# Every second weight unit issued by GpSimd through its own DMA queue, in a two-layer conv/MLA trunk with hierarchical MoE

## The chip, the cores and the metric

One core of a Trainium2 chip runs the whole kernel. The core has TensorE (PE in the profile; PEld is its weight load), VectorE (DVE), ScalarE (ACT), GpSimd (POOL) and SyncE (SP), each with its own instruction stream, and sixteen DMA engines that they share. The metric is the time of one execution on the device in microseconds; lower is better.

## What is computed

A token sequence of 256 by 1024 (float32) goes through two layers. Layer 0 is a Conformer convolution module, layer 1 an MLA attention over a shared latent. Each is followed by a mixture of 32 experts in 4 groups, of which a token uses two. The experts are nearly all of the weights, and every expert's weights are read:

```python
def hierarchical_moe(h, norm_g, w_group, b_group, w_router, b_router, w_gate_up, w_down):
    xt = rms_norm(h, norm_g).reshape(B * S, D)
    ...
    def expert_step(acc, ex):
        w_gu, w_d, g = ex
        a, b = jnp.split(xt @ w_gu, 2, axis=-1)
        return acc + ((jax.nn.silu(a) * b) @ w_d) * g[:, None], None

    y, _ = lax.scan(expert_step, jnp.zeros_like(xt), (w_gate_up, w_down, gates.T))
    return y.reshape(B, S, D)
```

`w_gate_up` is 32 x 1024 x 1024 in each layer and `w_down` 32 x 512 x 1024.

## The kernel before

The program is written by hand, engine by engine, with semaphores. Nothing is scheduled by a tool: the order of a queue is the order in the code.

*Units and slots.* The experts of a layer are taken four at a time; such a set is a quad, and there are eight. Each quad's weights come as twelve units of 2 MB: units 0 to 7 are gate_up, 8 to 11 are down. The units of a layer are numbered through, g = 0 to 95. They land in ten slots in SBUF, six in the tensor `ring` and four in `zone`; unit g takes the slot of unit g - 10 in turn. In the first quad, and for the down units of the last, a unit holds 128 weight rows of all four experts and comes in rows of 4 KB (`128x4x1024`). In all others ("blocks") it holds 512 rows of one expert, and each partition gets 16 KB that lie together (`128x4096`).

*Who frees a slot.* TensorE counts the semaphore `used` up. In the first quad it does so after each unit; in blocks it takes units in pairs (0 with 1, 2 with 3, ...) and adds two after a pair. `unit_free` waits for that count:

```python
sp.wait_ge(e["used"], UNITS * n + (u // 2 * 2 + 2 if blocks else u + 1))
```

*The order on SyncE.* Behind the inputs and the convolution's weights, `experts(l, first)` issues 84 units (`EARLY`) in order and then, in a loop `sp.Fori` over a count of rounds that is computed on the device (one, with this routing), the twelve units of the last quad. `first(g)` holds the first ten units back until the memory that they overwrite has been read. In the last quad, units 0 and 1 take the slots of units 6 and 7 of the quad before it, and units 6 and 7 those of this quad's units 0 and 1. Then come the attention weights (L445 to L451) and the same for layer 1.

*TensorE in a quad.* `gate_up` (L845), then `gather` for the next quad (L827), `hidden_across` and `weights_back` (L855, L863), `down` (L879) and `scatter` (L894). In the last quad `down` takes its units one by one.

*GpSimd.* It sets constants and adds up the products of the depthwise convolution (L506, L509). After that it has nothing to do for the rest of the kernel.

Of the kernel before, what the change touches and what calls it, by code (L numbers as in the profile page):

```python
# [14 lines left out]
P = 128  # L15
# [5 lines left out]
SIDE = 4  # L21
# [4 lines left out]
SLOTS = 10  # L26


def trunk_kernel(nc: bass.Bass, a, out):
    _, S, D = a["x"].shape  # L30
    L, NE, _, FF2 = a["w_gate_up"].shape
    F = FF2 // 2
    TT = S // P
# [15 lines left out]
    QUADS = NE // SIDE  # L49
    ROUNDS = QUADS * (PASSES - 1) + 1  # L50
    HALF = 512
    assert TT == 2 and D == 2 * HALF and NOPE == P and DV == P and QUAD == P and KF * P == F and NE == 32

    with ExitStack() as ctx:
        def sb(name, shape, dt=F32):
            return ctx.enter_context(nc.sbuf_tensor(name, shape, dt))

        def sem(name):
            return ctx.enter_context(nc.semaphore(name))
# [7 lines left out]
        unit_sb = [(ring[:, u * UNIT:(u + 1) * UNIT] if u < 6 else zone[:, (u - 6) * UNIT:(u - 5) * UNIT])  # L67
                   .rearrange("p (k c) -> p k c", k=4) for u in range(SLOTS)]
# [60 lines left out]
        slot = sb("slot", [P, TT, NC_])  # L129
        cmx = sb("cmx", [P, 1 + PASSES])  # L130
        rounds_i = sb("rounds_i", [P, 1], I32)
# [60 lines left out]
        def added_count(j):  # L192

            return j + 1 + block_of_buffered[j]

        def sums_done(b):

            return block_of_buffered.index(b) + block_of_buffered.count(b) + b + 1

        def product_buf(i):  # L200

            return spot(2304 + i * S, S) if i < 6 else spot(UNIT + 2048 + (i - 6) * S, S)
# [30 lines left out]
        for loads, at, parts in (  # L233
# [8 lines left out]
            first = at  # L242
# [10 lines left out]
        GU = KD  # L253
        UNITS = KD + KF
        EARLY = UNITS * (QUADS - 1)
# [5 lines left out]
        def slot_of(l, g):  # L261

            return slot_order[l][g % SLOTS]

        def slot_last(l, u):

            return slot_order[l][turn_last[u]]
# [7 lines left out]
        def by_blocks(n):  # L275

            return n != 0
# [49 lines left out]
        pw1_done, sg_ready, u_ready, u_zero = sem("pw1_done"), sem("sg_ready"), sem("u_ready"), sem("u_zero")  # L327
# [3 lines left out]
        mean_done, diff_ready = sem("mean_done"), sem("diff_ready")  # L331
        sq_ready, var_done, lstd_ready, dn_ready = sem("sq_ready"), sem("var_done"), sem("lstd_ready"), sem("dn_ready")
        c_ready, pw2_done, hb_ready = sem("c_ready"), sem("pw2_done"), sem("hb_ready")
# [3 lines left out]
        mask_ready, pos_done, rounds_ready = sem("mask_ready"), sem("pos_done"), sem("rounds_ready")  # L337
        count_done = sem("count_done")

        E = []  # L340
        for l in range(L):
            e = {n: sem(f"{n}_{l}") for n in (
                "gate_done", "used", "half_done", "pick_ready", "pw_ready", "g_done", "xs_ready", "silu_done", "hid_ready",
                "hT_done", "hidT_ready", "back_done", "pwT_ready", "y_ready", "s_done", "s_added")}
# [4 lines left out]
        ang_ready, trig = sem("ang_ready"), sem("trig")  # L349
        c_done, csq, crms_ready, cn_ready = sem("c_done"), sem("csq"), sem("crms_ready"), sem("cn_ready")  # L350
        ctr_done, cT_ready = sem("ctr_done"), sem("cT_ready")
        kvmm_done, kv_evac, qmm_done, q_evac = sem("kvmm_done"), sem("kv_evac"), sem("qmm_done"), sem("q_evac")
# [6 lines left out]
        o_done, o_dve, o_act, wo_done = sem("o_done"), sem("o_dve"), sem("o_act"), sem("wo_done")  # L359
# [6 lines left out]
        def _(sp):  # L366
# [31 lines left out]
            def unit_dma(l, slot, u, ex, blocks):  # L398
                src = a["w_gate_up"][l] if u < GU else a["w_down"][l]
                if blocks:  # L400
                    r0 = (u // SIDE) * HALF if u < GU else 0
                    src = src[bass.ds(ex + u % SIDE, 1), r0:r0 + HALF, :].rearrange("e (p k) c -> (e p) k c", k=4)
                else:
                    r0 = (u if u < GU else u - GU) * P
                    src = src[bass.ds(ex, SIDE), r0:r0 + P, :].rearrange("e p c -> p e c")
                sp.dma_start(unit_sb[slot], src).then_inc(E[l]["unit_in"][slot], 16)

            def unit_free(e, n, u, blocks):

                sp.wait_ge(e["used"], UNITS * n + (u // 2 * 2 + 2 if blocks else u + 1))  # L410

            def experts(l, first):
                e = E[l]
                for g in range(EARLY):
                    if g < SLOTS:
                        first(g)
                    else:
                        unit_free(e, (g - SLOTS) // UNITS, (g - SLOTS) % UNITS, by_blocks((g - SLOTS) // UNITS))
                    unit_dma(l, slot_of(l, g), g % UNITS, SIDE * (g // UNITS), by_blocks(g // UNITS))
                sp.wait_ge(rounds_ready, l + 1)  # L420
                n_last = sp.value_load(rounds_i[0:1, 0:1], min_val=1, max_val=ROUNDS)
                with sp.Fori(0, n_last) as i:
                    for u in range(UNITS):
                        if u in (6, 7):
                            unit_free(e, i + (QUADS - 1), u - 6, True)
                        else:
                            unit_free(e, i + (QUADS - 2), u + 6 if u < 2 else u, True)
                        unit_dma(l, slot_last(l, u), u, (i + (QUADS - 1)) % QUADS * SIDE, u < GU)
                return n_last

            def first_after_conv(g):
# [7 lines left out]
                if g == 8:  # L439
                    sp.wait_ge(pw2_done, 4)  # L440

            last = experts(0, first_after_conv) + (QUADS - 2)

            unit_free(E[0], last, 6, True)
# [8 lines left out]
            def first_after_attention(g):  # L453
# [6 lines left out]
                if g == 4:  # L460
                    sp.wait_ge(wo_done, 4)

            last = experts(1, first_after_attention) + (QUADS - 2)
            out_t = out[0].rearrange("(t p) d -> p t d", p=P)
            for j in range(4):
# [6 lines left out]
        @block.gpsimd  # L472
        def _(pool):
            nc.gpsimd.memset(ident[:, :], 0.0).then_inc(zeroed, 1)
            nc.gpsimd.memset(upto[:, :], 1.0).then_inc(zeroed, 1)
            nc.gpsimd.memset(mask[:, :], 0.0).then_inc(zeroed, 1)
            pool.wait_ge(zeroed, 3)
            nc.gpsimd.affine_select(out=ident[:, :], in_=ident[:, :], compare_op=ALU.not_equal, fill=1.0, base=0,
                                    pattern=[[-1, P]], channel_multiplier=1).then_inc(const_ready, 1)
            nc.gpsimd.affine_select(out=upto[:, :], in_=upto[:, :], compare_op=ALU.is_ge, fill=0.0, base=0,  # L480
                                    pattern=[[1, P]], channel_multiplier=-1).then_inc(const_ready, 1)

            nc.gpsimd.memset(mask[0:CHUNK, S - CHUNK:S], -NEG).then_inc(const_ready, 1)
            nc.gpsimd.memset(ones[:, :], 1.0).then_inc(const_ready, 1)
            nc.gpsimd.memset(eps_c[:, :], EPS).then_inc(const_ready, 1)
            nc.gpsimd.memset(slot[:, :, :], -1.0).then_inc(const_ready, 1)
            nc.gpsimd.iota(iota_i[:, :], pattern=[[1, CAP]], base=0, channel_multiplier=0).then_inc(const_ready, 1)
            nc.gpsimd.memset(u_sb[:, :, 0:PAD], 0.0).then_inc(u_zero, 1)
            pool.wait_ge(small_in, 16)
            pool.wait_ge(xn_ready, 2)  # L490
            for t in range(TT):
                nc.gpsimd.tensor_tensor(h[:, t, :], h[:, t, :], pw2_b_row, ALU.add).then_inc(hb_ready, 1)

            pool.wait_ge(tr_done, 4)
            nc.gpsimd.memset(mean_w, 1.0 / D).then_inc(mean_set, 1)

            made, j = 0, 0
            for b, (m, acc, other, w0) in enumerate(SUMS):
                for i in range(CW - w0):
                    made += 1  # L500
                    if i >= 2:
                        pool.wait_ge(product_ready, made)
                        if i >= 4:
                            pool.wait_ge(pool_added, added_count(j - 2))
                        dst = acc if i % 2 == 0 else other
                        nc.gpsimd.tensor_tensor(dst, dst, product_buf(j % PRODUCTS), ALU.add).then_inc(pool_added, 1)  # L506
                        j += 1
                pool.wait_ge(pool_added, sums_done(b) - 1)
                nc.gpsimd.tensor_tensor(acc, acc, other, ALU.add).then_inc(pool_added, 1)  # L509


        @block.scalar
        def _(act):
# [20 lines left out]

            act.wait_ge(cols_ready, 1)
            made, diags = iter(range(sum(CW - w0 for _, _, _, w0 in SUMS))), iter(range(CW))
            made_buffered = [0]

# [936 lines left out]
```

## Time and profile before

| | |
|---|---|
| median of 3 runs | 1174.38 us (1172.61 to 1174.65) |
| the profiled execution | 1175.39 us, with a span of 1173.7 us from first to last instruction |
| mean granted TensorE clock | 0.971 |
| TensorE busy | 1055.6 us (90%) |
| VectorE, ScalarE, GpSimd busy | 243.8, 168.7, 58.2 us |
| transfers | 430.72 MB, 367 GB/s over the span |

The profile is of one execution. Its times count from the first instruction; what lies around the span, 1.69 us here, is in the execution's time alone. Busy time of an engine says how much it did, not whether the kernel waited for it; for that the stages and the chain of waits are read. Transfers are listed by queue (q1 holds what SyncE issues, q10 what ScalarE issues, q8 and q14 bring instructions).

### The profile page before, as it was taken

The page shows a single profiled execution, that of the slowest core. Times are in us where ns is not written, and L with a number is a line of the kernel's source. Part 1 is how long each engine was busy: PE and PEld are TensorE (multiplying, and loading weights), DVE is VectorE, ACT ScalarE, POOL GpSimd, SP SyncE. Part 2 cuts the span into 40 slices and gives each one's busy share as a digit, 9 for nine tenths or more (in the row PEclk, how much of TensorE's full clock was granted, in tenths as well). Part 3 has the DMA queues.
Part 4 walks back from the last instruction along what each step waited for, and adds up shares of the span by engine and source line. Part 5 has one row for each costly group of instructions (what it writes and reads, how often), then busy time and mean ns, then how long its engine had stood idle before and what let it go on. Part 6 is the DMA issues. An engine that isn't in the chain of part 4 may idle for free.

```text
span 1173.7 us, 11470 instructions
## 1 busy us (share of the span) xinstructions
PE 1055.6 (90%) x4866; PEld 505.6 (43%) x4866; DVE 243.8 (21%) x521; ACT 168.7 (14%) x427; POOL 58.2 (5%) x92
## 2 busy tenths in 40 slices
PE   6999799989898979898999897979898989798988
PEld 5885542424242424242555555424242424242424
DVE  4993411101010100010226314101010101010001
ACT  2775200000000000000236202000000000000000
POOL 2790000000000000000000000000000000000000
PEclk9999799999999999999999897999999999999999
DMA  9683599999999999999975009999999999999996
GB/s 320 183 359 143 215 383 428 428 427 428 429 427 429 428 428 427 428 428 421 385 298 215 1 1 369 421 428 428 428 428 427 427 428 427 428 427 429 427 422 277
DMA packets 63966, 430.72 MB, mean 367 GB/s; under 512 B 12086, under 2 KB 22413, under 8 KB 43180
## 3 DMA queue, kind: packets, MB, share of 16 engines
q1 hardware_dynamic: 63790, 429.86, 88.7%
q8 instruction: 38, 0.62, 0.2%
q10 hardware_dynamic: 126, 0.14, 0.0%
q14 instruction: 12, 0.10, 0.0%
HBM read 428.94 MB, written 1.05 MB: 366 GB/s over the span
## 4 chain that ended last, share of the span: by engine, by line
PE 55%; DMA 39%; DVE 3%; ACT 1%; issue 1%; SPq 0%; ACTq 0%; DVEq 0%
DMA zone<-in_w_gate_up_dram 21%; DMA ring<-in_w_gate_up_dram 18%; PE bank L845 13%; PE bank L827 11%; PE bank L879 10%; PE bank L745 5%; PE bank L1034 2%; PE bank L785 2%; PE bank L967 1%; PE bank L894 1%; PE bank L977 1%; PE bank L757 1%; PE bank L945 1%; ACT xT L610 1%; PE bank L951 1%
## 5 line engine op out<-in xcount | busy, mean ns | idle before, releaser
L845 PE MATMUL bank<-ring,zone 128*32 128x512 f32 x1184 | 327.9, 608 | 39.9 <-DMA ring<-in_w_gate_up_dram 25.9
L845 PE MATMUL bank<-zone 128*32 128x512 f32 x864 | 270.9, 613 | 33.5 <-DMA zone<-in_w_gate_up_dram 18.9
L845 PEld LDWEIGHTS bank<-ring,zone 128*32 128x32 f32 x1184 | 87.6, 112 | 216.2 <-issue 214.9
L879 PE MATMUL bank<-ring,xT 128*32 128x512 f32 x672 | 144.2, 593 | 4.2 <-ACT xT L610 4.2
L827 PEld LDWEIGHTS bank<-zone,xn 128*128 128x128 f32 x576 | 132.5, 324 | 14.1 <-issue 14.1
L845 PEld LDWEIGHTS bank<-zone 128*32 128x32 f32 x864 | 69.7, 113 | 158.9 <-issue 157.9
L827 PE MATMUL bank<-zone,xn 128*128 128x128 f32 x576 | 135.9, 398 | 0.5 <-DVE zone L1229 0.5
L1248 DVE TENSOR_TENSOR xT<-xT,bank 128x512 f32<-128x512 f32 x16 | 11.0, 688 | 474.5 <-PE bank L845 474.5
L879 PE MATMUL bank<-zone,xT 128*32 128x512 f32 x352 | 93.4, 594 | 3.3 <-ACT xT L610 3.3
L608 ACT ACTIVATE xT<-bank 128x512 f32<-128x512 f32 x16 | 9.6, 597 | 549.6 <-PE bank L845 549.6
L1253 DVE TENSOR_TENSOR h<-bank,h 128x512 f32<-128x512 f32 x64 | 44.3, 692 | 210.5 <-PE bank L894 210.5
L879 PEld LDWEIGHTS bank<-ring,xT 128*32 128x32 f32 x672 | 38.0, 110 | 78.2 <-issue 72.4
L894 PE MATMUL bank<-zone,xT 128*128 128x512 f32 x128 | 62.3, 618 | 0.0
L745 PE MATMUL bank<-xT,ring 128*128 128x256 f32 x256 | 58.1, 391 | 0.8 <-issue 0.8
L745 PEld LDWEIGHTS bank<-xT,ring 128*128 128x128 f32 x256 | 50.3, 197 | 8.5 <-issue 1.2
L1132 DVE SCALAR_TENSOR_TENSOR bank<-zone,dwT,bank 128x256 f32<-128x256 f32 x125 | 49.9, 482 | 0.0
L1241 DVE TENSOR_TENSOR zone<-bank,cols 128x512 f32<-128x512 f32 x36 | 24.9, 692 | 109.0 <-PE bank L827 109.0
L879 PEld LDWEIGHTS bank<-zone,xT 128*32 128x32 f32 x352 | 23.6, 110 | 46.2 <-issue 42.0
L618 ACT COPY zone<-bank 128x512 f32<-128x512 f32 x32 | 18.8, 586 | 163.3 <-PE bank L879 163.3
L894 PEld LDWEIGHTS bank<-zone,xT 128*128 128x128 f32 x128 | 20.3, 188 | 42.2 <-DVE h L1253 21.0
L506 POOL TENSOR_TENSOR xn<-xn,zone 128x256 f32<-128x256 f32 x41 | 29.5, 732 | 0.4 <-ACT zone L560 0.4
L1034 PE MATMUL bank<-ring,xT 128*128 128x512 f32 x64 | 27.9, 594 | 1.5 <-ACT xT L704 1.5
(238 smaller groups left out, 624.3 us busy)
## 6 DMA issues: line engine op xcount, KB each, us to landing
ring<-in_w_gate_up_dram SPq DMA_DIRECT2D x74, 2048.0 KB, 35.2
zone<-in_w_gate_up_dram SPq DMA_DIRECT2D x54, 2048.0 KB, 35.4
ring<-in_w_down_dram SPq DMA_DIRECT2D x42, 2048.0 KB, 34.9
zone<-in_w_down_dram SPq DMA_DIRECT2D x22, 2048.0 KB, 35.8
ring<-in_a_pw_w_dram SPq DMA_DIRECT2D x8, 1024.0 KB, 11.8
ring<-in_a_pw_w_dram SPq DMA_DIRECT2D x2, 2048.0 KB, 11.4
ring<-in_w_o_dram SPq DMA_DIRECT2D x1, 4096.0 KB, 23.4
ring<-in_w_uq_dram SPq DMA_DIRECT2D x1, 2304.0 KB, 13.0
```

Of the source, the lines that this page charges most:

```text
L506: nc.gpsimd.tensor_tensor(dst, dst, product_buf(j % PRODUCTS), ALU.add).then_inc(pool_added, 1)
L618: nc.scalar.copy(y_sb[:, b * HALF:(b + 1) * HALF], bank[2 + b][:, :]).then_inc(e["y_ready"], 1)
L745: ins = nc.tensor.matmul(bank[4 + m % 4][:, part * S:(part + 1) * S], pw1_sb[2 * (m // 2) + part][:, k, (m % 2) * P:(m % 2 + 1) * P], xT[: ...
L785: ins = nc.tensor.matmul(bank[4 + 2 * t + hf][:, :], cv[:, k, t * P:(t + 1) * P], pw2_sb[hf][:, k, :], start=(k == 0), stop=(k == KD - 1))
L827: ins = nc.tensor.matmul(bank[4 + k // 4][:, (k % 4) * QUAD:(k % 4 + 1) * QUAD], xn_by_row[:, t, k // 4, k % 4, :] if blocks else xn[:, t, ...
L845: ins = nc.tensor.matmul(bank[b][s * CAP:(s + 1) * CAP, :], xs[:, k, s * CAP:(s + 1) * CAP], rhs[:, b * HALF:(b + 1) * HALF], start=(k == ...
L879: ins = nc.tensor.matmul(bank[2 + b][s * CAP:(s + 1) * CAP, :], hidT[:, k, s * CAP:(s + 1) * CAP], rhs[:, b * HALF:(b + 1) * HALF], start= ...
L894: nc.tensor.matmul(bank[6 + j % 2][:, :], pwT[:, t * P:(t + 1) * P], y_sb[:, hf * HALF:(hf + 1) * HALF], start=True, stop=True).then_inc(e ...
L1034: ins = nc.tensor.matmul(bank[wo_bank(2 * t + hf)][:, :], oT[:, hh, t * P:(t + 1) * P], w_o_sb[:, hh, hf * HALF:(hf + 1) * HALF], start=(h ...
L1132: ins = V.scalar_tensor_tensor(out=cv[:, m, :] if w == (width - 1) // 2 * 2 else acc, in0=u_sb[:, m, w:w + S], scalar=dwT[:, m, w:w + 1], ...
L1241: V.tensor_tensor(xs[:, 4 * b:4 * b + 4, :], bank[4 + b][:, :].rearrange("p (k c) -> p k c", k=4), over(col(gain, 4 * b, 4), QUAD), ALU.mu ...
L1253: V.tensor_tensor(h[:, t, hf * HALF:(hf + 1) * HALF], bank[6 + j % 2][:, :], h[:, t, hf * HALF:(hf + 1) * HALF], ALU.add).then_inc(added, 1)
```

## The change

SyncE keeps the units with even numbers. GpSimd gets functions of the same names and issues the odd ones, with the same waits for slots, behind its convolution sums. Where a skipped unit had a `first` wait, the issuer of the next unit waits for that too, so that memory is still protected on both queues.

```diff
             def experts(l, first):
                 e = E[l]
-                for g in range(EARLY):
+                for g in range(0, EARLY, 2):
                     if g < SLOTS:
+                        if g > 0:
+                            first(g - 1)
                         first(g)
...
                 with sp.Fori(0, n_last) as i:
-                    for u in range(UNITS):
+                    for u in range(0, UNITS, 2):
...
+            def unit_dma(l, slot, u, ex, blocks):
...
+                pool.dma_start(unit_sb[slot], src).then_inc(E[l]["unit_in"][slot], 16)
+
+            def unit_free(e, n, u, blocks):
+
+                pool.wait_ge(e["used"], UNITS * n + (u // 2 * 2 + 2 if blocks else u + 1))
+
+            def experts(l, first):
+                e = E[l]
+                for g in range(1, EARLY, 2):
+                    if g < SLOTS:
+                        if g > 0:
+                            first(g - 1)
+                        first(g)
+                    else:
+                        unit_free(e, (g - SLOTS) // UNITS, (g - SLOTS) % UNITS, by_blocks((g - SLOTS) // UNITS))
+                    unit_dma(l, slot_of(l, g), g % UNITS, SIDE * (g // UNITS), by_blocks(g // UNITS))
+                pool.wait_ge(rounds_ready, l + 1)
+                n_last = pool.value_load(rounds_i[0:1, 0:1], min_val=1, max_val=ROUNDS)
+                with pool.Fori(0, n_last) as i:
+                    for u in range(1, UNITS, 2):
...
+            experts(0, first_after_conv)
+            experts(1, first_after_attention)
```

The two places that matter below are the start of layer 0's units and the last quad. This is SyncE at the start of layer 0 before the change, from unit 0 to unit 11; the last two rows are units 10 and 11's slots coming free (`used_0`), with unit 9 ahead of unit 10 in the row before:

```order
L406 DMA zone<-in_w_gate_up_dram 128x4x1024
L406 DMA ring<-in_w_gate_up_dram 128x4x1024 [waits pw1_done] x4
L406 DMA zone<-in_w_gate_up_dram 128x4x1024 [waits ang_ready,mean_done]
L406 DMA zone<-in_w_gate_up_dram 128x4x1024
L406 DMA ring<-in_w_gate_up_dram 128x4x1024 [waits pw2_done]
L406 DMA ring<-in_w_down_dram 128x4x1024 [waits pw2_done]
L406 DMA zone<-in_w_down_dram 128x4x1024
L406 DMA zone<-in_w_down_dram 128x4x1024 [waits used_0]
L406 DMA ring<-in_w_down_dram 128x4x1024 [waits used_0]
```

The same place on SyncE after the change, units 0, 2, 4, 6, 8 and 10:

```order
L406 DMA zone<-in_w_gate_up_dram 128x4x1024
L406 DMA ring<-in_w_gate_up_dram 128x4x1024 [waits pw1_done] x2
L406 DMA zone<-in_w_gate_up_dram 128x4x1024 [waits ang_ready,mean_done]
L406 DMA ring<-in_w_down_dram 128x4x1024 [waits pw2_done]
L406 DMA zone<-in_w_down_dram 128x4x1024 [waits used_0]
```

And on GpSimd after the change, where the last sums of the convolution stand ahead of units 1, 3, 5, 7, 9 and 11:

```order
L508 TENSOR_TENSOR xn<-xn,zone 128x256 [waits pool_added,product_ready] x11
L511 TENSOR_TENSOR xn<-xn 128x256 [waits pool_added]
L521 DMA ring<-in_w_gate_up_dram 128x4x1024 [waits pw1_done] x2
L521 DMA zone<-in_w_gate_up_dram 128x4x1024 [waits ang_ready,mean_done,pw1_done]
L521 DMA ring<-in_w_gate_up_dram 128x4x1024 [waits pw2_done]
L521 DMA zone<-in_w_down_dram 128x4x1024 [waits pw2_done]
L521 DMA ring<-in_w_down_dram 128x4x1024 [waits used_0]
```

The odd units have left SyncE's row of issues, and units 1 and 3 now come behind the sums. In the last quad of layer 0, this is what GpSimd has from unit 5 on (an ISA row that waits is `unit_free` with a count from a register), and behind the loop the first odd units of layer 1:

```order
L521 ISA [waits used_0]
L521 DMA ring<-in_w_gate_up_dram 128x4096
L525 ISA
L521 ISA [waits used_0]
L521 DMA zone<-in_w_gate_up_dram 128x4096
L525 REGISTER_ALU
L521 ISA [waits used_0]
L521 DMA ring<-in_w_down_dram 128x4x1024
L525 REGISTER_ALU
L521 ISA [waits used_0]
L521 DMA ring<-in_w_down_dram 128x4x1024
```

Units 5, 7, 9 and 11 stand here behind waits of their own; units 6, 8 and 10, which stood between them, are on SyncE.

## Rows read from the trace of the kernel before

**Rows 1.** The page: busy time (share) xinstructions by engine; DMA queues.

```profile
PE 1055.6 (90%) x4866; PEld 505.6 (43%) x4866; DVE 243.8 (21%) x521; ACT 168.7 (14%) x427; POOL 58.2 (5%) x92
...
q1 hardware_dynamic: 63790, 429.86, 88.7%
```

**Rows 2.** Stages: start:end, us, busy (xinstructions), granted clock, DMA share, GB/s.

```profile
0.00:29.00 29.00, 17.86 (x74) 15.45 (x75) 11.55 (x27) 7.49 (x16) 7.20 (x18) 1.00 1.01 320
...
88.00:146.00 58.00, 48.80 (x200) 31.87 (x198) 20.45 (x54) 22.82 (x39) 0.47 (x1) 0.88 0.47 181
...
165.00:555.00 390.00, 352.87 (x1614) 139.53 (x1614) 37.80 (x61) 18.12 (x36) 0.00 (x0) 0.98 1.01 427
...
645.00:704.00 59.00, 53.39 (x192) 30.72 (x193) 17.18 (x22) 11.10 (x39) 0.00 (x0) 0.94 0.00 1
...
750.00:1143.00 393.00, 353.40 (x1588) 137.13 (x1580) 37.09 (x60) 16.96 (x32) 0.00 (x0) 0.98 1.01 427
...
555.00:565.00 10.00, 1.00 1.03 409
```

**Rows 3.** The chain that ended last, 144 to 230 us: start, us, what.

```profile
146.19 13.94 PE bank L845 x128
...
210.21 7.66 PE bank L827 x32
...
226.12 0.33 SPq L406
...
226.49 33.53 DMA ring<-in_w_gate_up_dram
```

**Rows 4.** Waits of SyncE's queue and of TensorE: total us, times, longest.

```profile
SPq L406 <- PE bank L845: 520.3, 60, 28.4
...
PE bank L845 <- DMA ring<-in_w_gate_up_dram: 39.8, 21, 2.7
PE bank L845 <- DMA zone<-in_w_gate_up_dram: 32.0, 16, 2.8
```

**Rows 5.** The same chain where each layer's stream ends.

```profile
536.25 18.94 DMA zone<-in_w_gate_up_dram
...
555.33 7.06 PE bank L845 x32
562.39 7.67 PE bank L827 x32
...
571.24 7.07 PE bank L879 x64
...
1143.54 0.14 issue
...
1159.58 7.07 PE bank L879 x64
```

**Rows 6.** SyncE's issues by time (start, us held); then issues of 536.8:538 with landing.

```profile
41.53 5.12 SPq L391 DMA_DIRECT2D wr<-in_w_router_dram  x1
...
55.42 19.01 SPq L406 DMA_DIRECT2D ring<-in_w_gate_up_dram  x4
90.90 0.92 SPq L406 DMA_DIRECT2D zone<-in_w_gate_up_dram  x2
118.02 0.37 SPq L406 DMA_DIRECT2D ring<-in_w_gate_up_dram  x1
...
zone<-in_w_down_dram SPq DMA_DIRECT2D x1, 2048.0 KB, 23.5
...
ring<-in_w_down_dram SPq DMA_DIRECT2D x1, 2048.0 KB, 28.0
```

**Rows 7.** GpSimd's last instruction before the change, by time.

```profile
87.75 0.72 POOL L509 TENSOR_TENSOR xn<-xn 128x256 f32<-128x256 f32 x1
```

**Rows 8.** DMA queues in 260:283, then in 284:286: packets, MB, share of 16 engines.

```profile
q1 hardware_dynamic: 675, 9.83, 100.4%
...
q8 instruction: 1, 0.02, 3.3%
```

More of the change, by code:

```diff
@@ L509, in _ @@
                 nc.gpsimd.tensor_tensor(acc, acc, other, ALU.add).then_inc(pool_added, 1)
+            def unit_dma(l, slot, u, ex, blocks):
+                src = a["w_gate_up"][l] if u < GU else a["w_down"][l]
+                if blocks:
+                    r0 = (u // SIDE) * HALF if u < GU else 0
+                    src = src[bass.ds(ex + u % SIDE, 1), r0:r0 + HALF, :].rearrange("e (p k) c -> (e p) k c", k=4)
+                else:
+                    r0 = (u if u < GU else u - GU) * P
+                    src = src[bass.ds(ex, SIDE), r0:r0 + P, :].rearrange("e p c -> p e c")
+                pool.dma_start(unit_sb[slot], src).then_inc(E[l]["unit_in"][slot], 16)
@@ new lines, in unit_free @@
+            def unit_free(e, n, u, blocks):
[7 more added lines that the diff above has]
+                        first(g)
+                    else:
+                        unit_free(e, (g - SLOTS) // UNITS, (g - SLOTS) % UNITS, by_blocks((g - SLOTS) // UNITS))
[4 more added lines that the diff above has]
+                    for u in range(1, UNITS, 2):
+                        if u in (6, 7):
+                            unit_free(e, i + (QUADS - 1), u - 6, True)
+                        else:
+                            unit_free(e, i + (QUADS - 2), u + 6 if u < 2 else u, True)
+                        unit_dma(l, slot_last(l, u), u, (i + (QUADS - 1)) % QUADS * SIDE, u < GU)
+                return n_last
@@ new lines, in first_after_conv, with first_after_attention @@
+            def first_after_conv(g):
+                if 1 <= g < 5:
+                    pool.wait_ge(pw1_done, 2 * g)
+                if g == 5:
+                    pool.wait_ge(mean_done, 1)
+                    pool.wait_ge(ang_ready, 1)
+                if g == 7:
+                    pool.wait_ge(pw2_done, 3)
+                if g == 8:
+                    pool.wait_ge(pw2_done, 4)
+            def first_after_attention(g):
+                if g == 0:
+                    pool.wait_ge(c_done, 4)
+                if g == 1:
+                    pool.wait_ge(qmm_done, 6)
+                if g == 3:
+                    pool.wait_ge(kvmm_done, 8)
+                if g == 4:
+                    pool.wait_ge(wo_done, 4)
```

## Prediction

> **What bounds the kernel now.** I read the page's totals first: TensorE busy for 1055.6 us of 1173.7, and one DMA queue, q1, that takes 88.7% of the sixteen engines' time; GpSimd has 58.2 us of work [rows 1]. A share over the whole span doesn't say which of the two ends a wait, so next the stages. From 165 to 555 us and from 750 to 1143 us the DMA engines are full (share 1.01) and move 427 GB/s, with TensorE busy for 352.87 of 390 us; from 645 to 704 us no weights move at all [rows 2]. So there are two streams of weight units, one for each layer's experts, and each is bound by transfers: 2.097 MB at 428 GB/s is 4.90 us for a unit, 58.8 us for the twelve units of a quad, while TensorE works 58.8 x 352.87 / 390 = 53.2 us of that.
>
> The chain of waits agrees. In layer 0 a slot comes free at 226.12, SyncE issues, and the unit lands 33.53 us later: some seven units stand in the queue ahead of it, so neither the issue nor a short delay of it is what TensorE waits for [rows 3]. SyncE itself waits for slots for 520.3 us on gate_up's units alone, and costs nothing by that [rows 4]. TensorE waits 39.8 + 32.0 us for units, at most 2.8 us at a time [rows 4].
>
> The order of landings matters only where a stream ends. There the chain is: SyncE's issue at 536.25, once units 0 and 1 are used, 18.94 us until units 6 and 7 of the last quad have landed (555.19), then TensorE's last two units of gate_up (7.06), the gather (7.67), the transposes, and the down units (7.07 from 571.24); layer 1 has the same chain, with unit 7 landed at 1143.54 and the down units from 1159.58 [rows 5]. Behind unit 7 come the four down units, in rows of 4 KB, at 409 GB/s [rows 2], so 5.13 us each: SyncE's issues at 536.84 and 537.41 land 23.5 and 28.0 us later, at 560.3 and 565.4, the other two by that pace at 570.6 and 575.7 [rows 6]. TensorE takes 7.07 / 4 = 1.77 us a unit and comes to unit 11 at 576.5, 0.8 us after it landed.
>
> **The change, part by part.** It removes 96 of SyncE's 192 unit issues and adds the same 96 on GpSimd. No byte, matmul or slot wait goes away. (a) SyncE's issue time, 0.33 to 0.43 us a unit where it isn't held [rows 6], lies under a backlog of some 30 us: worth nothing, and without that cover at most 96 x 0.4 = 38 us. (b) GpSimd runs the convolution's sums first, and the last ends at 88.47 us [rows 7]. Units 1 and 3, which SyncE issued from 55.42 on, now start there, with 5 and 6 at 90.9: four units, 20.5 us at 409 GB/s, done by 111 us. Units 7 to 9 still go from 118 on [rows 6], and the first expert matmul is at 146.19 [rows 3]. From 88 to 146 us the DMA share is 0.47 [rows 2], so this costs nothing; without that slack it would be 10.3 us. No sum of GpSimd's stands behind a transfer. (c) Loop and register work of GpSimd in the last quad stands before issues whose data has at least 9 us of queue ahead (18.94 less two units of 4.90): hidden. (d) SyncE's loads of w_dq and what follows it lie behind the same bytes as before: nothing.
>
> (e) What is left is the order in which units land. Two queues on the same engines take turns, and I take the turns to be equal, since the pieces are (16 KB in both). Even and odd units then land as pairs, which suits gate_up, where TensorE takes units in pairs. In the last quad it takes the down units one by one: unit 10 now lands with 11 at 575.7, but is wanted at 571.24 + 2 x 1.77 = 574.8. That costs 0.9 us in layer 0; in layer 1, 1143.54 + 4 x 5.13 = 1164.1 against 1159.58 + 3.53 = 1163.1, 1.0 us.
>
> (f) The queues don't start together. SyncE may issue unit 10 when unit 0 of the first quad is used, GpSimd unit 11 when unit 1 is: 13.94 / 8 = 1.74 us later [rows 3]. To that comes d, by which GpSimd needs longer than SyncE from release to first byte. For these x us SyncE's queue has the engines alone; with equal turns it stays ahead by as much for the whole stream, as long as neither queue runs empty, so each odd unit lands x us later than in one queue. The stream ends no later, but unit 7 of the last quad is odd and heads the chain of rows 5, so layer 0 ends x later. No row shows a GpSimd transfer, so d is bounded: below by 0; above by the longest that an issue held SyncE in the small loads, 5.12 us (a 1024-piece load) [rows 6]. I take 0.7 us, a short GpSimd instruction (0.72) [rows 7], the nearest row. Layer 0 then loses 1.74 + 0.7 = 2.4 us, in which (e) is hidden. In layer 1 both queues are released by the same wait at 705 us, so only d leads; 0.7 is below the 1.0 us of (e), which stays.
>
> The sum: 1175.39 (the profiled run's own time, 1.69 over its span) + 2.4 + 1.0 = 1178.8. That run is 1.0 us above the median, so **1177.8 us**, 0.3% slower. With d = 0 it is 1.7 + 1.0, 1177.1. With d = 5.1 it is 6.8 + 5.1, at most 1186.3.
>
> [...]
>
> **The rivals.** *No change.* The queues may serve nearly in the order of issue, or the lead may close in one of the stretches in which TensorE gathers and frees no slot. Then (f) is gone and at most (e) is left: 0 to 1.9 us, 1174.4 to 1176.3. For it: on average seven units stand in one queue, three or four in each of two, and a gather with its transposes frees nothing for about 16 us (210.21 to 226.12) [rows 3], three units' time. Against it: even then each queue still holds about two. [...]
>
> *Faster.* Two queues might hide what an engine loses between pieces. A piece of 16 KB takes 16384 / (428 / 16) = 612 ns, one of 4 KB 160 ns at 409 GB/s; a fixed 9.5 ns each and a limit of 435 GB/s fit both. Hidden, that gives 1.5% of the 783 us in rows 2 at 427 GB/s, 12 us: 1163. TensorE with its 53.2 of 58.8 us would allow it. Against it: the share is already 1.01, so no engine stands still between pieces. It decides from about 430 GB/s up: the forecast's 3.4 us and 2.3 more are 0.7% of the streams.
>
> *A lower rate.* GpSimd's pieces may be 4 KB, or one of the sixteen engines may be slower with them; a unit has landed only when the last engine is done. At the rate of 4 KB pieces each of the 80 units in 16 KB pieces that moves to GpSimd takes 0.23 us more: +18, with the 3.4 above 1196. It decides over the forecast from 426 GB/s down. [...]
>
> [...]
>
> **How the numbers follow.** Forecast 0.37 (its own range 1177 to 1186), no change 0.27, faster 0.14, a lower rate 0.16, a dear change 0.06. The range is 1162 to 1198: it holds four cases and leaves out the dear change and the tails, some 0.1. What a measurement here can tell from no change is 0.2%, 2.3 us. Faster is the one case, 0.14; same 0.27; slower the other three, 0.59.
>
> **What would show it.** Two queues with 96 units each, pieces of 16384 bytes in both, and together 427 to 428 GB/s from 165 to 555 us. Units landing in pairs 9.8 us apart. The last gate_up pair of layer 0 starting at about 557.7 instead of 555.33, and that of layer 1 at most 1 us later relative to the stream's start; attention's length unchanged. GpSimd's first unit at about 89 us and the first expert matmul still at 146. The prediction is wrong if the rate in the streams moves by over 1 GB/s, if one queue runs far ahead of the other, or if the DMA share falls below 1.0 in the middle of a stream, for then a queue starved behind GpSimd.

## The result, and the profile after

| | before | after |
|---|---|---|
| median of 4 runs | 1174.52 us (1172.61 to 1175.69) | 1197.92 us (1193.43 to 1200.22) |
| ratio | | 1.0196, 95% interval 1.0164 to 1.0229 |
| the profiled execution | 1175.39 us, span 1173.7 | 1198.17 us, span 1196.4 |
| mean granted TensorE clock | 0.971 | 0.955 |

The kernel became 2% slower, 23 us where 3.4 were forecast. First the page of the kernel after: two of its queue lines (packets, MB, share of sixteen engines' time) and the issues of units (count, KB, median us from issue to landing).

```profile
q1 hardware_dynamic: 43822, 228.53, 47.3%
q0 software_dynamic: 19968, 201.33, 40.1%
...
ring<-in_w_gate_up_dram SPq DMA_DIRECT2D x38, 2048.0 KB, 20.2
ring<-in_w_gate_up_dram POOLq DMA_DIRECT2D x36, 2048.0 KB, 39.9
zone<-in_w_gate_up_dram POOLq DMA_DIRECT2D x28, 2048.0 KB, 39.0
zone<-in_w_gate_up_dram SPq DMA_DIRECT2D x26, 2048.0 KB, 21.7
```

GpSimd's queue carries half of the units: 96 x 2.097 = 201.3 MB. But its units need 39 to 40 us from issue to landing where SyncE's need 20 to 22; the one queue of before needed about 35. The difference is 17 to 20 us, in a stream that lands a unit each 4.9 us.

The chain of the kernel after (start, us, what) at the head of layer 0's stream and at its end. L906 is gate_up, L888 the gather, L940 down, L955 scatter, L521 GpSimd's wait for a slot.

```profile
146.37 13.94 PE bank L906 x128
...
173.06 39.24 DMA zone<-in_w_gate_up_dram
...
212.43 8.40 PE bank L906 x32
...
538.46 7.02 PE bank L906 x38
...
545.50 0.04 POOLq L521
...
546.10 12.87 DMA zone<-in_w_gate_up_dram
...
559.10 8.76 PE bank L906 x32
...
576.71 7.07 PE bank L940 x64
```

The first expert matmul stands where it did, 146.37 against 146.19 [rows 3], so the late start of units 1 and 3 costs nothing. The second quad's first pair starts at 212.43, in the kernel before at 201.45; by 538.46 TensorE is still 9.9 us late (528.57 before): the issue that heads the last wait is made at 546.10, where it was at 536.25 [rows 5]. The wait behind it shrinks from 18.94 to 12.87 us, and the last pair of gate_up starts 3.8 us later (559.10 against 555.33), takes 8.76 us instead of 7.06 because a part of it lies at a lower level of TensorE's clock (from 560 to 565 us the granted clock is 0.67, where the kernel before has 1.00 from 555 to 565; from 555 to 560 us TensorE had 1.72 us of work with the clock at 0.99), and the down units start 5.5 us later (576.71 against 571.24).

Windows of the kernel after (columns as in [rows 2]): the stream of layer 0, three short stretches near its end, and attention.

```profile
165.00:555.00 390.00, 349.26 (x1613) 138.22 (x1614) 37.78 (x61) 18.12 (x36) 21.04 (x39) 0.98 1.00 422
510.00:515.00 5.00, 5.00 (x24) 2.45 (x21) 0.69 (x1) 0.60 (x1) 0.53 (x1) 1.00 0.80 308
515.00:520.00 5.00, 5.00 (x23) 5.00 (x22) 0.69 (x1) 0.00 (x0) 1.06 (x2) 1.00 0.90 351
545.00:550.00 5.00, 5.00 (x36) 1.40 (x31) 0.00 (x0) 0.00 (x0) 2.01 (x3) 1.00 0.72 229
645.00:704.00 59.00, 53.41 (x174) 31.24 (x173) 19.63 (x27) 13.28 (x41) 0.00 (x0) 0.71 0.05 20
```

The stream lost 5 of 427 GB/s over 390 us, 4.6 us of transfer time, and it lost them in holes: 308, 351 and 229 GB/s. In the first of them, from 512 to 514 us, SyncE's queue moves nothing and GpSimd's fills half of the engines' time (512.0 to 513.8 us: 0.41 MB, share 53.5%): SyncE issues its next unit at 513.84, once a slot is free. The last line holds the other half of the result. In attention, where next to no weights move (20 GB/s, 1 before), the mean granted clock is 0.71 where it was 0.94 [rows 2]. Here are three lines of the chain of the kernel after, two of its score matmuls (128x256) and the last gate_up pair of layer 1:

```profile
658.48 1.15 PE bank L1066 x2
...
675.73 1.16 PE bank L1067 x2
...
1164.42 8.56 PE bank L906 x32
```

and one of the chain of the kernel before, score matmuls of the same shape:

```profile
652.20 0.63 PE bank L1006 x2
```

At the lower level of the clock, 0.50 in this execution from 655 to 675 us, two of them take 1.15 us; at 1.00, in the kernel before from 643 to 660 us, 0.63. The scores run from 649.08 to 676.89 in the kernel after, 27.8 us, and from 643.61 to 660.37 before, 16.8: 11.0 us more, in work that the change doesn't touch. These are windows of TensorE around the start of the scores (us, busy, granted clock, DMA share, GB/s), first in the kernel before:

```profile
635.00:640.00 5.00, 4.19 (x39) 1.00 0.80 297
640.00:645.00 5.00, 4.24 (x34) 1.00 0.31 126
645.00:650.00 5.00, 5.00 (x25) 1.00 0.00 0
```

and in the kernel after:

```profile
640.00:645.00 5.00, 4.19 (x37) 1.00 0.57 186
645.00:650.00 5.00, 4.24 (x36) 1.00 0.58 237
650.00:655.00 5.00, 5.00 (x19) 0.71 0.00 0
```

TensorE was busy for the same 4.19 and 4.24 of 5 us ahead of both, and for all of the 5 us behind; in one the clock stayed at 1.00 and in the other it fell to half (0.71 from 650 to 655 us, 0.50 from 654 to 658), so its busy time just before doesn't tell the two apart. In layer 1 the last pair starts at 1164.42 and down at 1181.83, 22.25 us later than before. The shifts of the two chains add up: 0.2 (start) + 5.3 (layer 0) + 11.0 (clock in attention) + 5.7 (layer 1) = 22.2; the spans differ by 22.7, the rest being behind the last down units.

### The profile page after: what moved, and what is told of

The parts are those of the page before. It is cut to its first block, busy times and chain, and to the rows that moved or that the text cites. A ratio compares the mean times of both kernels' runs of the same rounds, so it can differ in the third digit from the quotient of the medians.

```text
span 1196.4 us, 11504 instructions
## 1 busy us (share of the span) xinstructions
PE 1063.5 (89%) x4866; PEld 508.0 (42%) x4866; DVE 243.7 (20%) x521; ACT 168.8 (14%) x427; POOL 112.6 (9%) x188
## 4 chain that ended last, share of the span: by engine, by line
PE 56%; DMA 39%; DVE 2%; ACT 1%; issue 1%; ACTq 0%; POOLq 0%; DVEq 0%
DMA zone<-in_w_gate_up_dram 21%; DMA ring<-in_w_gate_up_dram 17%; PE bank L906 13%; PE bank L888 11%; PE bank L940 10%; PE bank L806 5%; PE bank L1095 2%; PE bank L846 2%; PE bank L1028 1%; PE bank L955 1%; PE bank L1067 1%; PE bank L1066 1%; PE bank L1038 1%; PE bank L818 1%; PE bank L1006 1%
## 5 line engine op out<-in xcount | busy, mean ns | idle before, releaser
L906 PE MATMUL bank<-ring,zone 128*32 128x512 f32 x1184 | 324.8, 608 | 47.4 <-DMA ring<-in_w_gate_up_dram 29.7
L906 PE MATMUL bank<-zone 128*32 128x512 f32 x864 | 265.8, 613 | 30.2 <-DMA zone<-in_w_gate_up_dram 18.2
L906 PEld LDWEIGHTS bank<-ring,zone 128*32 128x32 f32 x1184 | 87.2, 112 | 223.9 <-issue 222.8
L940 PE MATMUL bank<-ring,xT 128*32 128x512 f32 x672 | 147.7, 615 | 13.7 <-DMA ring<-in_w_down_dram 9.5
L888 PEld LDWEIGHTS bank<-zone,xn 128*128 128x128 f32 x576 | 132.1, 323 | 14.1 <-issue 14.1
L888 PE MATMUL bank<-zone,xn 128*128 128x128 f32 x576 | 135.5, 397 | 0.5 <-DVE zone L1290 0.5
L906 PEld LDWEIGHTS bank<-zone 128*32 128x32 f32 x864 | 68.5, 113 | 151.0 <-issue 150.0
L940 PE MATMUL bank<-zone,xT 128*32 128x512 f32 x352 | 93.4, 594 | 3.3 <-ACT xT L671 3.3
L940 PEld LDWEIGHTS bank<-ring,xT 128*32 128x32 f32 x672 | 38.2, 112 | 89.7 <-issue 72.8
L521 POOL DMA_DIRECT2D ring<-in_w_gate_up_dram x36 | 20.5, 570 | 456.4 <-PE bank L906 165.6
L955 PE MATMUL bank<-zone,xT 128*128 128x512 f32 x128 | 62.9, 623 | 0.0
L521 POOL DMA_DIRECT2D zone<-in_w_gate_up_dram x28 | 15.2, 544 | 305.5 <-PE bank L906 218.6
L940 PEld LDWEIGHTS bank<-zone,xT 128*32 128x32 f32 x352 | 23.6, 110 | 46.2 <-issue 42.1
L955 PEld LDWEIGHTS bank<-zone,xT 128*128 128x128 f32 x128 | 20.6, 190 | 44.1 <-DVE h L1314 21.0
```

The lines of the kernel that those rows point to most:

```text
L521: pool.dma_start(unit_sb[slot], src).then_inc(E[l]["unit_in"][slot], 16)
L888: ins = nc.tensor.matmul(bank[4 + k // 4][:, (k % 4) * QUAD:(k % 4 + 1) * QUAD], xn_by_row[:, t, k // 4, k % 4, :] if blocks else xn[:, t, ...
L906: ins = nc.tensor.matmul(bank[b][s * CAP:(s + 1) * CAP, :], xs[:, k, s * CAP:(s + 1) * CAP], rhs[:, b * HALF:(b + 1) * HALF], start=(k == ...
L940: ins = nc.tensor.matmul(bank[2 + b][s * CAP:(s + 1) * CAP, :], hidT[:, k, s * CAP:(s + 1) * CAP], rhs[:, b * HALF:(b + 1) * HALF], start= ...
L955: nc.tensor.matmul(bank[6 + j % 2][:, :], pwT[:, t * P:(t + 1) * P], y_sb[:, hf * HALF:(hf + 1) * HALF], start=True, stop=True).then_inc(e ...
```

## Where the two units of lead come from

The trace's queues in 158 to 170 us, the head of the stream in the kernel after (packets, MB, share):

```profile
q1 hardware_dynamic: 273, 3.95, 77.5%
q0 software_dynamic: 274, 1.12, 22.8%
```

273 packets against 274, and 3.5 times the bytes. Of these 547 packets 306 are under 8 KB, and 32 of those under 512 B. So GpSimd's 274 are pieces of 4 KB (1.12 MB), and SyncE's are 241 pieces of 16 KB (3.95 MB) and 32 small ones, which are counted with the pieces from here on. In this stretch GpSimd's queue is at unit 11, which still belongs to the first quad and comes in pieces of 4 KB, while SyncE's is through with unit 10 (landed at 157.7) and at units 12 and 14, in pieces of 16 KB (unit 12 lands at 164.0, unit 11 at 177.4). The theory that the runs test is that the DMA engines take a piece from each queue in turn, whatever its size: while the pieces differ SyncE's queue runs ahead by two units, 9.8 us; once they are equal nothing takes that lead away, since each queue then gets half the bytes (from 260 to 283 us SyncE's moves 4.90 MB in 332 packets and GpSimd's 4.95 MB in 334). TensorE takes units in pairs, so it waits for the late odd one, and frees its slots 9.8 us late. In the stream this is hidden, as the queues are full; in the last quad it empties them.

The 273 against 274 agree with turns one for one. A second issuer costs some 11 us in these runs: 5.3 in layer 0 and 5.7 in layer 1.

## The experiments

Ratios are against the kernel before, run beside the experiment on the same chip. One thing is needed to read the medians: the executions of nearly every kernel, before too, fall in two groups by time and mean granted clock; those of the kernel before are 1172.3 to 1176.0 us with 0.969 to 0.974, and 1183.7 to 1187.6 with 0.957 to 0.961. The size fits the stretch of attention at half clock seen above (0.50 from 654 to 680 us, 0.71 and 0.87 in the windows 650 to 655 and 680 to 704): half the clock for 30 us lowers the mean over 1175 us by 15/1175 = 0.013. I call them executions at full and at half clock in attention; for the profiled ones it was read from the trace, for the others it is inferred from these two numbers. Where a median mixes them, both groups are given. No execution of the kernel before at half clock was profiled.

**gate12**: the lead taken from SyncE's queue at its source.

```diff
+                    if g == 12:
+                        sp.wait_ge(e["unit_in"][slot_of(l, 11)], 32)
                     unit_dma(l, slot_of(l, g), g % UNITS, SIDE * (g // UNITS), by_blocks(g // UNITS))
```

> The changed kernel with one more wait in each layer: SyncE issues unit 12 only once unit 11 has landed, so that SyncE has no 16 KB pieces in its queue while GpSimd's still moves unit 11 in 4 KB pieces. Theory (the engines take one piece from each queue in turn, and SyncE's lead of two units comes from the stretch in which its pieces are four times as large): the lead is at most some 3 us, gate_up's last pairs start at most 4 us later than in the kernel before instead of 9.8, layer 0 ends at most 3 us later instead of 5.5, and the run is at 1176 to 1184 us if attention keeps the full clock, 11 us more if it doesn't. Rival (SyncE's queue is favoured over GpSimd's as such): the lead of two units is back within a quad or two, the pairs are 9.8 us late again, and the run is at 1195 to 1200 us.

Measured: median 1186.11 us of 10 runs, ratio 1.0063 (1.0017 to 1.011); four runs at full clock, 1175.9 to 1178.6, five at half, 1188.9 to 1191.1, and one between, 1183.29. From its page:

```profile
ring<-in_w_gate_up_dram SPq DMA_DIRECT2D x38, 2048.0 KB, 35.9
ring<-in_w_gate_up_dram POOLq DMA_DIRECT2D x36, 2048.0 KB, 30.4
```

and from its chain at the end of layer 0's stream (L908 is gate_up, L942 down):

```profile
553.55 8.76 PE bank L908 x32
...
571.16 7.07 PE bank L942 x64
```

One wait at the head of a stream of 96 units takes SyncE's lead away for all of it, and turns it round: GpSimd's units now land 5 to 8 us sooner after their issue than SyncE's. Layer 0's down units start at 571.16, where before the change it was 571.24. That is in part the luck of this execution, whose first expert matmul came 2.1 us early, at 144.13; measured from there layer 0 still takes 2.0 us more than before the change, against 5.3 in the changed kernel. The expectation (at most 3 us; 1176 to 1184 us at full clock) held, and SyncE's queue isn't favoured. But the profiled execution had half clock in attention (granted clock 0.71 from 645 to 704 us), without SyncE's lead and with layer 0 on time: the clock is a matter of its own.

**hold10**: the mirror. SyncE's unit 10 is held back, so that GpSimd's unit 11 may go first.

```diff
                         unit_free(e, (g - SLOTS) // UNITS, (g - SLOTS) % UNITS, by_blocks((g - SLOTS) // UNITS))
+                        if g == 10:
+                            sp.wait_ge(e["used"], 5)
```

> The changed kernel with one more wait in each layer: SyncE issues unit 10 only when five units of the first quad are used, about 7 us later, so that now GpSimd is the first to reach 16 KB pieces while SyncE still moves unit 10 in 4 KB pieces. Theory (one piece from each queue in turn): the lead turns round, odd units land about two units ahead of even ones, GpSimd's time from issue to landing becomes the short one (about 20 us) and SyncE's the long one (about 39), and the run stays near 1198 us. Rival (SyncE's queue is favoured): SyncE leads as in the changed kernel, 20 us against 39 the same way round.

Measured: median 1192.25 us of 10 runs, ratio 1.0114 (1.0071 to 1.0158); three at 1179.9 to 1184.2 with a clock of 0.962 or 0.963, one at 1187.18, six at 1192.1 to 1197.1 with 0.956 or less. Its queues in 158 to 170 us:

```profile
q0 software_dynamic: 274, 3.97, 77.9%
q1 hardware_dynamic: 272, 1.11, 22.7%
```

and a line of its page:

```profile
ring<-in_w_gate_up_dram POOLq DMA_DIRECT2D x36, 2048.0 KB, 26.2
```

The two queues have changed places: again 274 pieces against 272, and now GpSimd's has 3.6 times the bytes. So it is the size of the pieces at that moment, not the engine that issues. The rest of the expectation came out only in part: the latencies are 26.2 us on GpSimd's queue and 37.0 on SyncE's for the same tensor, not 20 and 39, and the time is below 1198, since layer 0 lost 6.4 us but layer 1 only 1.2. Why the lead cost so little in layer 1 wasn't followed up.

**allpool**: all expert units on GpSimd, none on SyncE; one queue, as before, but the other one.

```diff
-                for g in range(0, EARLY, 2):
+                for g in ():
...
-                for g in range(1, EARLY, 2):
+                for g in range(EARLY):
```

> All 192 units on GpSimd's queue in one order, none on SyncE's. Theory (nothing is wrong with GpSimd's transfers, only two queues side by side get out of step): the streams move at 427 GB/s, units land 4.9 us apart in order, no pair is late, and the run is within 3 us of the kernel before (1174 to 1178 us). [...]

Measured: median 1190.7 us of 4 runs (1183.55 to 1194.85), ratio 1.0109 (1.0047 to 1.0171). The window of layer 0's stream:

```profile
165.00:555.00 390.00, 357.29 (x1608) 138.84 (x1610) 37.77 (x61) 18.12 (x36) 41.81 (x78) 0.97 1.01 427
```

and two lines of its page:

```profile
ring<-in_w_gate_up_dram POOLq DMA_DIRECT2D x74, 2048.0 KB, 35.0
zone<-in_w_gate_up_dram POOLq DMA_DIRECT2D x54, 2048.0 KB, 35.3
```

427 GB/s and 35 us, as with SyncE: GpSimd's queue is not slower. The time of 1174 to 1178 us that this was to give didn't come. Beside the clock in attention, what the kernel loses is at the end of layer 0, where SyncE, with no units to issue, sends the attention weights beside the last units; its chain ends in a wait of 39.88 us for a down unit, and attention starts at 589.53 instead of 585.41 (6.0 us later when measured from the first expert matmul). Three of its four executions (0.955 to 0.958) were at half clock, the fourth (1183.55, 0.967) was not.

**shift24**: the kernel before, with 24 idle matmuls ahead of attention's projections, to see whether a later attention alone brings the half clock.

```diff
+            for _ in range(24):
+                nc.tensor.matmul(bank[6][:, 0:S], ident[:, :], xT[:, 0, :], start=True, stop=True)
```

> The kernel before, with 24 matmuls of 128x256 more on TensorE between the expert stage of layer 0 and attention, about 5.5 us of busy TensorE; their result is overwritten by the next matmuls. Theory (the clock's halving in attention depends only on when attention falls, and the 5.5 us by which layer 0 ended later in the changed kernel bring it on): the score matmuls run at half clock, attention takes some 11 us more, and the run is at 1190 to 1192 us. Rival (the clock fell for another cause that only the changed kernel has): attention keeps its length and the run is at 1179 to 1181 us.

Measured: median 1185.05 us of 10 runs, ratio 1.0089 (1.0064 to 1.0115); nine at 1183.1 to 1186.95 with a clock of 0.968 or more, one at 1194.78 (0.957). The added matmuls took 10.60 us, twice what I had expected, and with layer 0 ending 1.7 us early in this execution attention's end moved by 8.7 us. The window of attention in its profile:

```profile
645.00:704.00 59.00, 51.84 (x229) 33.18 (x228) 23.50 (x32) 17.17 (x48) 0.00 (x0) 0.94 0.09 35
```

The granted clock is 0.94, as in the kernel before. A theory of mine fell here, that any shift of attention by some us puts it at the lower clock. The shift was 9 us, though, and one of exactly 5.5 us, as in the changed kernel, wasn't run.

**l0only and l1only**: GpSimd takes the odd units in one layer alone; in the other SyncE issues all, as before.

```diff
-                for g in range(0, EARLY, 2):
+                for g in range(0, EARLY, 2 if l == 0 else 1):
...
             experts(0, first_after_conv)
-            experts(1, first_after_attention)
```

> GpSimd issues odd units in layer 0 only; in layer 1 SyncE issues all of them, as in the kernel before. Theory (the two queues out of step cost each layer by itself): layer 0 ends 5 to 6 us later as in the changed kernel, layer 1's stream and tail are as in the kernel before; with the full clock in attention the run is at 1180 to 1182 us, with the halved stretch 11 us more. For the clock: if the halving comes more often whenever GpSimd's queue has been used at all, more than half of the runs lie at 1190 to 1193; if it needs GpSimd's transfers of units 1 and 3 during attention, nearly all lie at 1180 to 1182.

> GpSimd issues odd units in layer 1 only; in layer 0 SyncE issues all of them, as in the kernel before. Theory: layer 0 and the start of attention are as in the kernel before, layer 1 ends some 6 us later; with the full clock in attention 1180 to 1182 us, with the halved stretch 11 us more. For the clock: if it needs GpSimd's transfers of units 1 and 3 during attention, more than half of the runs lie at 1190 to 1193; if the halving depends on how late layer 0 ends, nearly all lie at 1180 to 1182.

Measured: layer 0 alone, median 1187.85 us of 12 runs, ratio 1.0077 (1.0036 to 1.0119); five at 1177.6 to 1180.9, seven at 1186.9 to 1194.1. Layer 1 alone, median 1180.64 of 12, ratio 1.0026 (0.9997 to 1.0056), with the clock between 0.964 and 0.970 in all twelve. That ratio says little, because the runs of the kernel before beside these were themselves of both kinds, 14 at 1172.4 to 1175.3 (0.971 or more) and 9 at 1183.7 to 1187.6 (0.960 or less). Against the 14 the loss is some 6 us. The end of l1only's chain shows it (L939 is down):

```profile
1127.72 7.02 PE bank L905 x38
...
1135.37 12.89 DMA zone<-in_w_gate_up_dram
1148.39 8.53 PE bank L905 x32
...
1165.78 7.07 PE bank L939 x64
```

The same 12.9 us of wait and the same 8.5 us pair as in the changed kernel; down starts 6.2 us later than before (1159.58), of which 0.7 came from ahead. In l0only's profile layer 0 takes 4.5 us more than before, a little less than expected, and layer 1 no more. Each layer pays for its own lead. And the 9 runs point to the half clock in attention in the kernel before, too, so that 7 of 12 for l0only says nothing of the clock.

**again and gate14**: the changed kernel in more executions, and a gate two units later than gate12's, after unit 12, which is to bring the queues level instead of turning the lead.

```diff
+                    if g == 14:
+                        sp.wait_ge(e["unit_in"][slot_of(l, 11)], 32)
                     unit_dma(l, slot_of(l, g), g % UNITS, SIDE * (g // UNITS), by_blocks(g // UNITS))
```

> The changed kernel once more, unaltered, in more executions, to tell its two parts apart. Theory (the change itself costs some 11 to 12 us, through SyncE's queue leading by two units in both streams, and the rest of the 23 us is a stretch of attention at the half clock that befalls only a part of the executions, as it befell 12 of 48 of the kernel before): the times fall into two groups, one at 1186 to 1188 us with a granted clock of about 0.965 and one at 1197 to 1200 us at about 0.955, and the layer 0 stream ends 5.5 us later than before in either. Rival (the stall at the end of the layer 0 stream always brings the half clock into attention): all executions at 1196 to 1200 us.

> The changed kernel, with SyncE waiting before unit 14 of each layer until unit 11 has landed. Nothing else is altered; no work is left out. Theory (the two queues give their pieces in turn, so that the lead of two units that SyncE's queue wins while GpSimd's unit 11 has 4 KB pieces lasts until something takes it away): the lead goes, but less is overturned than with the wait before unit 12, issue to landing is 30 to 38 us on both queues, the last expert work of layer 0 ends within 1.5 us of the kernel before (at about 571 us), and the time where attention keeps its clock is 1175 to 1179 us. Rival (a lead comes back in the following 80 units whatever is done at their start, since SyncE issues sooner than GpSimd): latencies far apart again, about 20 and 40 us, and 1186 us at the least.

Measured, again: median 1197.37 us of 6 runs, ratio 1.0176 (1.014 to 1.0213); five at 1197.2 to 1197.9 with a clock of 0.950 to 0.956, one at 1188.31 with 0.963. So the half clock seems not to come always with the change, and without it the time is 1188, some 14 us more than the kernel before at full clock. The two chains above account for 11 of these (5.5 + 5.7); that execution has no profile to tell the rest. The profiled one is at half clock, and its down units in layer 0 start at 576.25, 5.0 us later than before the change.

gate14: median 1180.11 us of 11 runs, ratio 1.005 (1.0026 to 1.0073); ten at 1177.9 to 1181.1, one at 1190.85 (0.957). From its page:

```profile
ring<-in_w_gate_up_dram SPq DMA_DIRECT2D x38, 2048.0 KB, 35.0
ring<-in_w_gate_up_dram POOLq DMA_DIRECT2D x36, 2048.0 KB, 39.7
```

Its window of layer 0's stream:

```profile
165.00:555.00 390.00, 357.39 (x1614) 140.26 (x1613) 37.75 (x61) 18.10 (x36) 21.04 (x39) 0.98 1.01 427
```

Its chain at the end of that stream:

```profile
537.36 38.21 DMA ring<-in_w_down_dram
575.62 3.64 PE bank L942 x32
579.26 3.84 PE bank L957 x8
```

The lead is gone, and with it the holes (427 GB/s, share 1.01). For gate_up's units in `zone` the two queues need 38.8 and 38.1 us, for those in `ring` 35.0 and 39.7, where 30 to 38 were expected; the times at full clock are 1 to 2 us over the expected 1175 to 1179 us as well, but clear of the rival's 1186. The chain no longer runs over the last gate_up pair: it ends with the down units, which now land together at 575.6, so the scatter ends 0.9 us later than before, at 583.10 against 582.16. In layer 1 the scatter starts 4.6 us later than before (1171.29 against 1166.65); 3.1 of these were there at attention's end (709.07 against 705.94), the 0.9 and 2.2 us of a value matmul group that took 16.16 us instead of 13.97, its first 4 us at a low clock (0.50 from 670 to 675 us), and 1.5 arose in layer 1. The lead did not come back in the 80 units that followed the gate: of the units issued from 480 to 520 us, those of SyncE take 25.9 and 39.7 us to land and those of GpSimd 25.9 and 39.6.

The profiled executions come to their first expert matmul at different times, 144.13 to 146.84 us, which blurs any comparison by absolute time. Here is each stage by itself, in us more than in the kernel before, from the chains of one execution each: layer 0 from its first expert matmul to its last scatter, then to layer 1's first expert matmul (in it attention), then to layer 1's last scatter.

| | first expert matmul at | layer 0 | attention stage | layer 1 |
|---|---|---|---|---|
| before | 146.19 | (432.13) | (147.72) | (440.61) |
| after | 146.37 | +5.3 | +11.0 | +5.7 |
| again | 145.99 | +5.2 | +11.1 | +5.6 |
| gate12 | 144.13 | +2.0 | +11.0 | +2.4 |
| hold10 | 144.33 | +6.4 | +11.1 | +1.2 |
| allpool | 144.33 | +6.0 | +11.2 | +0.9 |
| shift24 | 144.53 | 0.0 | +10.3 (the added matmuls: 10.6) | 0.0 |
| l0only | 144.45 | +4.5 | -0.2 | -0.3 |
| l1only | 146.84 | +0.1 | 0.0 | +5.5 |
| gate14 | 146.00 | +1.1 | +2.2 | +1.5 |

## Why the prediction was right, and where its sizes were off

The direction was right, and for half of the loss so was its cause, a queue that leads. That the time lies in the range is luck: 1197.92 is 0.1 us inside its upper end of 1198, and that end was drawn for GpSimd's pieces moving at a lower rate, which they don't. The forecast's own range, 1177 to 1186, was missed, and half of the loss is a clock that no term had. By the signs that the prediction gave for being wrong it was wrong on how the change works: the rate in layer 0's stream moved by 5 GB/s, one queue ran far ahead of the other, and the DMA share fell to 0.80 and 0.72 near the stream's end. The forecast was made of small terms, and the largest was too small.

*(a), (c), (d), what costs nothing.* Right as far as seen: GpSimd takes 0.53 to 0.74 us for a single issue, and no wait of the chain in the middle of a stream is for an issue.

*(b), units 1 and 3 later.* Right: GpSimd's first issue stands at 88.60, the first expert matmul at 146.37.

*(e), pairs instead of single landings, 0.9 and 1.0 us.* Right where the queues are level, about: gate14 has its down units of layer 0 landed together at 575.6 (575.7 was forecast) and shows 0.9 in layer 0 (1.1 from the first expert matmul on) and 1.5 in layer 1.

*(f), the lead of one queue.* This is the step that failed, in two places. It rests on (e), which said "I take the turns to be equal, since the pieces are (16 KB in both)", and it priced the lead by the late start alone, 1.74 + d us. The turns are equal in pieces, 273 against 274, but the pieces aren't equal when the lead is made: unit 11 comes in 4 KB and units 12 and 14 in 16 KB. The lead was 2 units, 9.8 us, beyond even the bound, 1.74 + 5.1 = 6.8. The code told of it: the first quad comes in rows of 4 KB, as the description of the units says, and I didn't use that in the sum. What the prediction said of a lead once won was right: it lasts for the whole stream. The other place is "The stream ends no later". With a lead of two units the slots come free so late in the last quad that the queues run out: the holes of 4.6 us in layer 0. Hence it was the last pair's 3.8 us later start and its 1.7 us at the lower clock that made 5.5, and not x = 2.4; in layer 1, 5.7 instead of 1.0.

*d, from release to first byte.* It was taken as 0.7 us. At the head of layer 1's stream both queues are empty, and both engines issue (time, us held):

```profile
721.81 0.37 SPq L406 DMA_DIRECT2D ring<-in_w_gate_up_dram  x1
722.03 0.74 POOL L521 DMA_DIRECT2D ring<-in_w_gate_up_dram  x1 [80.66 <-PE bank L1095]
```

In the kernel after, the queues in 722 to 723 us and in 726 to 727 us, the first windows of 1 us in which each moves a piece:

```profile
q1 hardware_dynamic: 4, 0.02, 10.8%
...
q1 hardware_dynamic: 84, 0.34, 85.9%
q0 software_dynamic: 11, 0.05, 13.9%
```

SyncE's first piece comes 1 us after the issue, GpSimd's some 4 us. So d is about 3 us, inside its bounds, and the lead of 9.8 covers it.

*"Attention's length unchanged".* Wrong, by 11 us, half of the measured loss. By time and clock the half clock came in 13 of 65 executions of the kernel before (those run beside the experiments) and in 9 of 10 of the kernel after. The experiments ran in three sets on three chips, and the kernel before has it at different rates in them, so only counts of one set can be compared. Beside 3 of 25 of the kernel before: gate12 5 of 10, hold10 6 of 10, allpool 3 of 4, shift24 1 of 10. Beside 1 of 17: the kernel after again 5 of 6, gate14 1 of 11. Beside 9 of 23: l0only 7 of 12 (one of them, 1186.91 us with 0.963, by its time alone), l1only 0 of 12. So the kernel after, gate12, hold10 and allpool have it more often than the kernel before beside them, and gate14, with level queues, doesn't. Whether layer 0 is what matters isn't shown: l0only's 7 of 12 can't be told from 9 of 23. All this is a link by counts, and no mechanism: a later attention alone doesn't bring it (shift24, 9 us), and gate12 has it with attention starting on time. What lowers the clock there stays open.

The rivals: *no change* fell, *faster* too (no run moved more than 427 GB/s over layer 0's stream). *A lower rate* came out in the average, 422, but not by its mechanism: allpool and gate14 move 427 with GpSimd's pieces, and the loss lies in holes. *A dear change*, a piece that costs more wherever the queue changes, to which the forecast gave 0.06, has no row that shows such a cost, and the runs show none: from 260 to 283 us 666 packets of the two queues (9.86 MB) fill 100.7% of the engines' time in the kernel after, where 675 of one queue (9.83 MB) filled 100.4% [rows 8], and gate14, with two queues throughout, moves 427.

So the 23 us are: about 5.5 and 5.7 from the lead and the holes that it tears, which gate14 shows by taking them away, and 11 from a clock that fell in attention in most executions, for a reason not found. No version here is faster than the kernel before; gate14, with two queues in both layers the best by its median, is 0.5% slower. The four executions of gate12 at full clock, 1175.9 to 1178.6 us, are shorter than gate14's, but half of gate12's are at half clock.

## What to carry to other kernels

Splitting one in-order stream over two queues gave nothing here, where the DMA engines were full (share 1.01 before), and it gave up the order. The queues shared the engines by pieces (3.95 against 1.12 MB at 273 against 274): before you call two queues equal, compare the sizes of the pieces that stand side by side in them, at the head of the stream above all, since a lead won there lasted to the end. If a stream must be split, try to make the queues level with one wait right behind the unequal pieces; where it stands matters, as gate12 and gate14 show. And when executions are compared, compare stages from a common start. A median that holds two groups of executions has to be taken apart by the granted clock before any ratio is explained.

## What the runs showed that I had not expected

The queues got their bytes by piece count: 3.95 against 1.12 MB in 12 us at 273 against 274 pieces, and the mirror, 1.11 against 3.97 MB, with the queues' parts changed. A queue of GpSimd moved 427 GB/s alone, as much as SyncE's, and needed some 3 us longer from issue to first byte. The score matmuls, which no variant alters, ran at a granted clock of 1.00 in some profiles and of 0.50 in others, 0.63 or 1.15 us for two of 128x256, and the times of one and the same program fell in two groups 11 us apart that fit this.
